# A decoder step on one core: twenty sample tokens taken out of the dense expert pass instead of sixteen, gate maps one to a chunk, and a shared projection for two query heads

## The chip, the cores and the metric

The kernel is one program on one core of one Trainium2 chip. The metric is the device time of one execution in microseconds (us); it is given as the median of the runs. The profile is one further execution, recorded by the hardware profiler. Its span runs from the first to the last instruction. All data are float32.

## What is computed

One layer of a decoder for two groups that share weights: 256 prompt tokens and 8 requests of 8 sample tokens, 320 tokens of width 2048 in all. Two attention mixers run side by side and share one output projection; cross-attention into 256 memory tokens follows; then the expert mixer, which takes more than half of the time. Cut to that mixer, for a block xb of tokens:

```python
q = (xb @ w_pq).reshape(TOKEN_BLOCK, PEER_HEADS, PEER_DKEY)        # 8 heads, 256 wide
s1 = jnp.einsum('thd,kd->thk', q[..., :half], sub_k1)              # 128 scores
s2 = jnp.einsum('thd,kd->thk', q[..., half:], sub_k2)
v1, i1 = lax.top_k(s1, PEER_TOPK); v2, i2 = lax.top_k(s2, PEER_TOPK)   # 16 and 16
cand = (v1[..., :, None] + v2[..., None, :]).reshape(..., PEER_TOPK * PEER_TOPK)
cidx = (i1[..., :, None] * PEER_NKEYS + i2[..., None, :]).reshape(...)
best, pos = lax.top_k(cand, PEER_TOPK)
eidx = jnp.take_along_axis(cidx, pos, axis=-1)                     # 16 of 16384 experts
gate = jax.nn.softmax(best.astype(jnp.float32), axis=-1)
act = jax.nn.gelu(jnp.einsum('td,thkd->thk', xb, expert_u[eidx]), approximate=False)
return jnp.einsum('thk,thkd->td', (gate * act).astype(xb.dtype), expert_v[eidx])
```

A token needs 8 x 16 = 128 experts, each a row of 2048 numbers (8 KB) in expert_u and one in expert_v. A residual add and a final RMSNorm close the layer. The outputs are both groups' results and the updated key and value buffers.

## The kernel before

It is written in raw blocks, one instruction list for each engine: SP issues the weight loads, POOL (GpSimd) the cache loads and the gathers, and PE, ACT and DVE compute. The order on each engine is the order of the code. Engines meet at counting semaphores: `x.wait_ge(s, n)` holds up that engine's whole list.

**Two token groups.** FIRST_TILE is the first 128 tokens; THE_REST is the other 192. **Weights** are streamed in pieces of 1 MB (128 x 2048 numbers) through `WR`, a ring of four slots. PE multiplies 16 stationary tiles of 128 x 128 out of each piece. A piece is loaded into its slot as soon as PE has used the piece that was there.

**Stages in order.** The memory projection and the input projection of all 320 tokens. Prompt attention in 16 steps, one pair of heads a step (`step_p` on DVE, `exp_p` and `turned_p` on ACT, `turn_p` on PE), over two probability buffers. Sample attention, one request after another (`softmax_s`, `turn_s`, `values_s`), with the output projection of FIRST_TILE, its cross-attention and its `co` tiles between the requests; at each request DVE adds the finished tiles to the stream (`add_to_stream`) after that request's softmax. Then the same stages for THE_REST (`out_tile`, `cq_tile`, its cross-attention over steps `it`, `co_tile`), with the query projection `pq_tile(0, f)` of FIRST_TILE between them. The order of tiles, and of the weight pieces with them, is the list `TILES`. A tile of `pq` for FIRST_TILE has 128 columns and one for THE_REST 192, and each `pq` piece is loaded twice. The memory keys and values of the requests are loaded by SP between weight pieces (`mem_keys`, `mem_values`): 2 MB of keys and 2 MB of values for requests 0 to 3, and as much again for 4 to 7.

**The expert mixer, by two methods.** For FIRST_TILE the chosen experts are gathered. One gather by POOL brings a "row": 128 expert rows, one to a partition, 1 MB. DVE takes its dot product with the tokens in `h_tok` (`u_dot`) or adds it, weighted, to the stream (`v_row`). There are 128 rows for these tokens (`SLOTS`) and, for the first `FEW` = 16 tokens of THE_REST, 16 more. So `ROWS` = 144 rows of expert_u and then 144 of expert_v go through rings of three buffers (`URING`) and four (`VRING`). For the other `DENSE` = 176 tokens every expert is computed: 128 chunks of 128 experts, with 16 matmuls each (`dense_u`, 176 columns wide) and a GELU by ACT, and then 128 chunks of expert_v (`dense_v`). Between the two, each token's gates are multiplied in. For four tokens at a time DVE writes one-hot matrices (`one_hots`), ACT weighs them, PE makes four gate maps (`gate_maps`), DVE applies the map to the chunks that are done (`apply_gates`), and ACT copies the rest (`s_gcp`).

**What stands where.** ACT's loop `dense_gelu` runs to chunk `EXPS` = 64 and takes the exponentials of the gates there; it runs on to `TAIL` = 80, where ACT waits for the gates and issues 8 small loads that spread the few tokens' choices over the partitions; then to `MAP_LO` = 100. PE has four output banks in turn, so that chunk c waits for the GELU of chunk c - 4. PE transposes the choices at chunk `TURN` = 92. DVE does 141 rows (`ROWS_BEFORE`) ahead of the gate maps, with a part of the choice of experts (`choose_part`, 18 parts for THE_REST) every third row from row 50 on. The 44 maps fall in chunks 100 to 123 (`chunk_of`). From chunk 100 on DVE does two rows at every third chunk and one at the others (`rows_with`).

The lines that open each half of the expert mixer for DVE:

```python
def u_dot(n):
    dve.wait_ge(s_ug[n % URING], 16 * (n // URING + 1))
def v_row(n):
    dve.wait_ge(s_vg[n % VRING], 16 * (n // VRING + 1))
```

## Time and profile before

| | us |
|---|---|
| median of 3 runs | 2312.56 (2309.89 to 2315.29) |
| the profiled execution | 2311.11 |
| its span | 2309.2 |
| PE busy, share of the span | 96% |
| DVE busy | 51% |
| bytes moved | 843.21 MB, mean 365 GB/s |

The profiled execution spends 1.9 us outside its span and lies 1.45 us below the median of the runs. A busy PE does not say that PE sets the pace: its matmuls overlap, and their ends are modelled. The number of instructions in a stretch says more. A float32 matmul stands as two instructions in the trace, so a piece of weights, or a chunk, is 32 of them. The stages in the trace: input projection until 397 us, prompt attention until 463, sample attention until about 660, THE_REST's projections and cross-attention until 905, its query projection until 997, chunks of expert_u until 1659 (the gate maps from 1485 to 1640), chunks of expert_v until 2293, and the final sums.

### The profile page before, as it was taken

The page shows a single profiled execution, that of the slowest core. Times are in us where ns is not written, and L with a number is a line of the kernel's source. Part 1 is how long each engine was busy: PE and PEld are TensorE (multiplying, and loading weights), DVE is VectorE, ACT ScalarE, POOL GpSimd, SP SyncE. Part 2 cuts the span into 40 slices and gives each one's busy share as a digit, 9 for nine tenths or more (in the row PEclk, how much of TensorE's full clock was granted, in tenths as well). Part 3 has the DMA queues.
Part 4 walks back from the last instruction along what each step waited for, and adds up shares of the span by engine and source line. Part 5 has one row for each costly group of instructions (what it writes and reads, how often), then busy time and mean ns, then how long its engine had stood idle before and what let it go on. Part 6 is the DMA issues. An engine that isn't in the chain of part 4 may idle for free.

```text
span 2309.2 us, 35404 instructions
## 1 busy us (share of the span) xinstructions
PE 2207.9 (96%) x14282; PEld 2015.7 (87%) x14282; DVE 1179.1 (51%) x2095; ACT 301.2 (13%) x926; POOL 386.3 (17%) x414
## 2 busy tenths in 40 slices
PE   7999998789889879999999999999999999999998
PEld 5677776577589868999999999899999999999998
DVE  3200003833566647767777544599744444444422
ACT  2000001722221012011111110144200000000000
POOL 0100000022302011232212221133311111111100
PEclk9999999999999989999999999999999999999999
DMA  7999982289959898999999999999999999999974
GB/s 280 405 413 381 385 316 81 80 333 357 398 201 396 345 383 315 407 398 422 422 421 420 420 420 420 372 372 376 402 422 421 422 422 421 422 422 422 421 315 155
DMA packets 117787, 843.21 MB, mean 365 GB/s; under 512 B 14432, under 2 KB 16608, under 8 KB 30656
## 3 DMA queue, kind: packets, MB, share of 16 engines
q1 hardware_dynamic: 62752, 485.30, 52.4%
q0 software_dynamic: 54128, 354.58, 37.7%
q10 hardware_dynamic: 816, 2.11, 0.2%
q8 instruction: 58, 0.95, 0.2%
q14 instruction: 33, 0.27, 0.0%
HBM read 834.25 MB, written 74.78 MB: 394 GB/s over the span
## 4 chain that ended last, share of the span: by engine, by line
PE 64%; DMA 23%; DVE 8%; issue 2%; ACT 1%; POOL 1%; SPq 0%; DVEq 0%; POOLq 0%; ACTq 0%
PE low L1414 39%; PE big L1414 24%; DMA BIG<-expert_u,VB 20%; DVE BIG L1240 4%; DMA WR<-wall 1%; DMA BIG<-kaT 1%; ACT BIG L630 1%; DMA BIG<-expert_v,VB 1%; DMA BIG<-memT 0%; DMA BIG<-va 0%; DVE CST L968 0%; POOL BIG L525 0%; DVE BIG L846 0%; PE low L1538 0%; DVE HT L883 0%
## 5 line engine op out<-in xcount | busy, mean ns | idle before, releaser
L1414 PE MATMUL low<-HT,WR 128*128 128x176 f32 (+3 forms) x6336 | 1081.9, 333 | 8.4 <-DMA WR<-wall 7.0
L1414 PEld LDWEIGHTS low<-HT,WR 128*128 128x128 f32 x6336 | 984.2, 191 | 98.2 <-issue 9.7
L1414 PE MATMUL big<-BIG,WR 128*128 (+3 forms) x2888 | 450.7, 312 | 11.3 <-DVE XT L891 7.1
L1253 DVE SCALAR_TENSOR_TENSOR XT<-BIG,VB,XT 128x2048 f32<-128x2048 f32 x128 | 300.9, 2351 | 302.7 <-DMA BIG<-expert_v,VB 302.4
L1414 PE MATMUL low<-BIG,WR 128*128 (+3 forms) x2616 | 434.8, 321 | 12.6 <-DMA WR<-wall 10.3
L1414 PEld LDWEIGHTS big<-BIG,WR 128*128 128x128 f32 x2888 | 419.3, 193 | 30.1 <-issue 18.5
L1240 DVE SCALAR_TENSOR_TENSOR BIG<-BIG 128x2048 f32<-128x2048 f32 x144 | 329.5, 2291 | 210.8 <-DMA BIG<-expert_u,VB 209.7
L1414 PEld LDWEIGHTS low<-BIG,WR 128*128 128x128 f32 x2616 | 411.0, 192 | 17.8 <-issue 10.5
L539 POOL DMA_INDIRECT BIG<-expert_u,VB x144 | 161.5, 1122 | 683.8 <-DVE BIG L1240 609.5
L545 POOL DMA_INDIRECT BIG<-expert_v,VB x144 | 161.5, 1122 | 558.2 <-DVE XT L1253 477.3
L914 DVE TENSOR_SCALAR BIG<-low 128x320 f32 x32 | 15.7, 492 | 264.0 <-PE low L1414 264.0
L1414 PE MATMUL big<-BIG 128*32 128x256 f32 (+4 forms) x868 | 80.5, 376 | 16.1 <-issue 8.9
L1414 PEld LDWEIGHTS big<-BIG 128*32 128x32 f32 (+2 forms) x868 | 52.7, 141 | 36.5 <-issue 14.6
L777 ACT ACTIVATE BIG<-low 128x176 f32 x100 | 31.8, 318 | 334.3 <-PE low L1414 324.2
L819 ACT ACTIVATE HT<-XT 128x2048 f32<-128x2048 f32 x1 | 1.9, 1910 | 557.1 <-DVE XT L1253 557.1
L793 ACT ACTIVATE HT<-HT,VB 128x128 f32<-128x128 f32 x176 | 56.2, 390 | 89.9 <-DVE HT L1354 89.9
L1354 DVE TENSOR_TENSOR HT<-CST,VB 128x512 f32<-128x512 f32 x88 | 56.6, 684 | 7.7 <-PE big L1414 7.7
L1414 PE MATMUL big<-HT 128*128 128x128 f32 x352 | 47.9, 280 | 5.0 <-ACT HT L793 5.0
L1414 PEld LDWEIGHTS big<-HT 128*128 128x128 f32 x352 | 45.5, 194 | 5.6 <-issue 5.5
L511 POOL DMA_DIRECT2D HT<-kbT x1 | 0.5, 536 | 266.8 <-PE low L1414 266.8
L525 POOL DMA_DIRECT2D BIG<-kaT x56 | 29.8, 539 | 81.2 <-PE low L1414 81.2
L622 ACT ACTIVATE BIG<-low 128x512 f32<-128x512 f32 (+3 forms) x5 | 2.3, 466 | 293.3 <-PE low L1500 293.3
(230 smaller groups left out, 1124.0 us busy)
## 6 DMA issues: line engine op xcount, KB each, us to landing
WR<-uT SPq DMA_DIRECT2D x128, 1024.0 KB
WR<-expert_v SPq DMA_DIRECT2D x128, 1024.0 KB
WR<-wall SPq DMA_DIRECT2D x122, 1024.0 KB
BIG<-va POOLq DMA_DIRECT2D x48, 512.0 KB, 11.0
BIG<-kaT POOLq DMA_DIRECT2D x64, 384.0 KB, 11.0
BIG<-kmT SPq DMA_DIRECT2D x2, 2048.0 KB, 12.9
BIG<-vm SPq DMA_DIRECT2D x8, 512.0 KB, 13.4
XT<-xT SPq DMA_DIRECT2D x1, 2560.0 KB, 21.9
```

The source lines that it names most:

```text
L525: pool.dma_start(kr[j][:, NEWK:SW], d["kaT"][n, j, :, FIRST:PAST]).then_inc(s_kr[j], 16)
L539: nc.gpsimd.indirect_dma_start(u_ring[n % URING], None, d["expert_u"], bass.IndirectOffsetOnAxis(eidx[:, n:n + 1], 0)).then_inc(s_ug[n % U ...
L545: nc.gpsimd.indirect_dma_start(v_ring[n % VRING], None, d["expert_v"], bass.IndirectOffsetOnAxis(eidx[:, v_slot(n):v_slot(n) + 1], 0)).the ...
L622: nc.scalar.activation(VT[0:m, t, q * 512:q * 512 + w], bank[3 + n % 2][0:m, 0:w], ACT.Copy).then_inc(s_vtev, 1)
L630: ins = nc.scalar.activation(pb[:, s, lo:hi], pb[:, s, lo:hi], ACT.Exp, bias=stat[:, c:c + 1], scale=1.0, accum_out=stat[:, c + 4:c + 5])
L777: nc.scalar.activation(C[:, bass.ds(i * (UB * DENSE) + r * DENSE, DENSE)], u_out[r], ACT.Gelu).then_inc(s_dev, 1)
L793: nc.scalar.activation(x, x, ACT.Copy, scale=turned[2][:, 4 * g + j:4 * g + j + 1]).then_inc(s_weighed, 1)
L914: nc.vector.tensor_scalar(QK[:, bass.ds(i * (4 * NT) + r * NT, NT)], bank[r % 2][:, 0:NT], 1.0, None, ALU.mult).then_inc(s_ev, 1)
L1240: nc.vector.scalar_tensor_tensor(out=u, in0=u, scalar=1.0, in1=h_tok if n < SLOTS else h_few, op0=ALU.mult, op1=ALU.mult, accum_out=dots[: ...
L1253: nc.vector.scalar_tensor_tensor(out=x_tok, in0=rows_of(row), scalar=weight, in1=x_tok, op0=ALU.mult, op1=ALU.add).then_inc(s_vsum, 1)
L1354: ins = nc.vector.tensor_tensor(hot[z][g % 2], iota.unsqueeze(1).broadcast_to([P, 4, NKEY]), turned[z][:, 4 * g:4 * g + 4].unsqueeze(2).br ...
L1414: return nc.tensor.matmul(out, lhsT, rhs, start=start, stop=stop, skip_group_check=True)
```

## The change

**More tokens gathered.** `FEWER` = 4 more tokens leave the dense pass: `DENSE` is 172 (`ALONE` = 20 tokens are gathered), and `ROWS` is 148. The 128 experts of each of the four tokens are laid out as four rows, with (quarter of the 16 choices, head, token) on the partitions. ACT issues four small loads for each head beside the one that was there: 40 in place of 8. Before row 144 PE transposes 16 blocks of the four tokens into `h_tok`, four blocks at each of chunks 92 to 95. The sums of the four go through `h_few` once more, after PE has added the first sixteen; that addition stands at V chunk 32 instead of 96, and the second one at 96. In the V half the four rows are rows 56 to 59.

**Gate maps.** They fall in chunks 80 to 122, one for each chunk after its last matmul, over three banks instead of four. `EXPS`, `TAIL` and `TURN` are 56, 64 and 72. DVE does 118 rows ahead of the maps, with two of the 18 parts in every five rows, and weighs the gates at row 98 instead of 106.

**Heads 6 and 7.** The four `pq` tiles 12 to 15 are computed for all 320 tokens at once, ahead of THE_REST's other twelve. Of the tiles 10 to 15 that stood in and behind the cross-attention of THE_REST, only 10 stands in it and 11 behind `co`.

**Memory loads.** The first keys and values are issued three weight pieces later; half of the second values get room of their own and go out with them.

**Prompt and sample attention.** DVE negates the row maxima (which lets ACT start its exponentials) ahead of the multiplications that normalize the pair before, and there is a third probability buffer from the sixth pair on. In the sample attention DVE adds the tiles that PE finished beside the scores ahead of the next softmax, and FIRST_TILE's `co` tiles from the seventh on rotate over three banks.

```diff
-EXPS, TAIL = 64, 80
-TURN = 92
-MAP_LO, MAP_HI = 100, 124
+EXPS, TAIL = 56, 64
+TURN = 72
+MAP_LO = 80
+E2_AT = 92
 MAPS = DENSE // 4
+MAP_HI = MAP_LO + MAPS
-ROWS_BEFORE = 141
+ROWS_WEIGH = 98
+ROWS_BEFORE = 118
...
-         + tiles_of("cq", 1, 0, 4) + tiles_of("pq", 0, 10, 14) + tiles_of("co", 1, 0, 16) + tiles_of("pq", 0, 14, 16)
-         + tiles_of("pq", 1, 0, 16))
+         + tiles_of("cq", 1, 0, 4) + tiles_of("pq", 0, 10, 11) + tiles_of("co", 1, 0, 16) + tiles_of("pq", 0, 11, 12)
+         + tiles_of("pq", 1, 12, 16) + tiles_of("pq", 1, 0, 12))
...
-                if before == POS["out", 1, 15]:
+                if before == POS["cq", 1, 0]:
                     sp.wait_ge(s_used, FREED["out", 1, 15])
                     mem_keys(0)
-                    mem_values(0)
+                    mem_values(0, 0, 4)
+                    sp.wait_ge(s_sc, 3)
+                    sp.wait_ge(s_idx, 3)
+                    mem_values(1, 0, 2)
...
             for h in range(PH):
-                act.dma_start(chosen[FEW * h:FEW * (h + 1), :, SLOTS:ROWS], few_src[:, :, h * PK:(h + 1) * PK]).then_inc(s_few, 16)
+                act.dma_start(chosen[FEW * h:FEW * (h + 1), :, SLOTS:SLOTS + FEW], few_src[:, :, h * PK:(h + 1) * PK]).then_inc(s_few, 16)
+                for part in range(PARTS):
+                    to, k = (part * PH + h) * FEWER, h * PK + part * FEWER
+                    act.dma_start(chosen[to:to + FEWER, :, SLOTS + FEW:ROWS], fewer_src[:, :, k:k + FEWER]).then_inc(s_few, 16)
...
-                if n + 1 < REQ:
-                    softmax_s(n + 1)
-                for f in (*with_scores, *with_turn):
+                for f in with_scores:
                     add_to_stream(FIRST_TILE, CROSS, f)
...
+                if n + 1 < REQ:
+                    softmax_s(n + 1)
+                for f in with_turn:
+                    add_to_stream(FIRST_TILE, CROSS, f)
...
-                if last:
-                    dve.wait_ge(s_dv, mr)
-                    nc.vector.tensor_scalar(pl[:, 0, 0:256], pl[:, 0, 0:256], rd[:, 0:1], None, ALU.mult)
-                    nc.vector.tensor_scalar(pl[:, 0, 256:384], pl[:, 0, 256:384], rd[:, 1:2], None, ALU.mult).then_inc(s_nrm, 1)
...
-                if n % 3 == 0 and later:
+                if (n - ROWS_AHEAD) % 5 in (0, 2) and later:
                     choose_part(*later.pop(0))
...
+            v_chunks(MAP_LO, FEWER_OUT)
+            pe.wait_ge(s_vsum, FEWER_AT + FEWER)
+            for k in range(KT):
+                mm(v_all[k][:, FEW:ALONE], h_few[:, k * P:(k + 1) * P], pick_fewer, start=False, stop=True)
+            v_chunks(FEWER_OUT, NCH - WR_N)
```

The small loads on ACT, in the row of the list at `TAIL`. Before:

```order
L777 ACTIVATE BIG<-low 128x176
L774 REGISTER_ALU
L774 COMPARE_AND_BRANCH
L786 DMA VB<-HT 16x2x16 x8
L774 UNCONDITIONAL_BRANCH
```

After:

```order
L813 ACTIVATE BIG<-low 128x172
L810 REGISTER_ALU
L810 COMPARE_AND_BRANCH
L822 DMA VB<-HT 16x2x16
L825 DMA VB<-HT 4x2x4 x4
```

The last two rows stand eight times in a row before the next loop of GELUs, where one row of eight loads stood.

SP's loads from the output projection to the first chunk of expert_u: weight pieces (`WR<-wall`), memory keys (`kmT`) and values (`vm`). Before:

```order
L484 DMA WR<-wall 128x2048 x51
L460 DMA BIG<-kmT 128x4x1024
L464 DMA BIG<-vm 128x1024 x4
L484 DMA WR<-wall 128x2048 x7
L460 DMA BIG<-kmT 128x4x1024
L484 DMA WR<-wall 128x2048 x2
L464 DMA BIG<-vm 128x1024 x4
L484 DMA WR<-wall 128x2048 x20
```

After:

```order
L517 DMA WR<-wall 128x2048 x54
L490 DMA BIG<-kmT 128x4x1024
L494 DMA BIG<-vm 128x1024 x6
L517 DMA WR<-wall 128x2048 x4
L490 DMA BIG<-kmT 128x4x1024
L517 DMA WR<-wall 128x2048
L494 DMA BIG<-vm 128x1024 x2
L517 DMA WR<-wall 128x2048 x17
```

Weight pieces come to 76 instead of 80, the first memory loads stand three pieces later, and two of the second four values stand ahead of the second keys.

PE from the last `co` tile of THE_REST to the first chunks of expert_u (`low<-HT,WR` are `pq` tiles, 16 matmuls to a tile). Before:

```order
L1414 MATMUL low<-HT,WR 128x128 x16
L1414 MATMUL big<-BIG,CST 128x192
L1414 MATMUL low<-HT,WR 128x128 x16
L1414 MATMUL big<-CST,BIG 128x128 x4
L1414 MATMUL low<-HT,WR 128x192 x32
L1766 MATMUL big<-CST,BIG 128x128 x16
L1414 MATMUL low<-HT,WR 128x192 x224
L1414 MATMUL low<-CST,BIG 128x128 x8
L1414 MATMUL big<-CST,BIG 128x128 x16
L1414 MATMUL low<-HT,WR 128x176 x64
```

After:

```order
L1472 MATMUL big<-BIG,CST 128x192
L1472 MATMUL low<-HT,WR 128x128 x16
L1472 MATMUL big<-CST,BIG 128x128 x4
L1472 MATMUL low<-HT,WR 128x320 x32
L1829 MATMUL big<-CST,BIG 128x128 x16
L1472 MATMUL low<-HT,WR 128x320 x32
L1472 MATMUL low<-HT,WR 128x192 x32
L1472 MATMUL big<-CST,BIG 128x128 x4
L1472 MATMUL low<-HT,WR 128x192 x160
L1472 MATMUL low<-CST,BIG 128x128 x8
L1472 MATMUL big<-CST,BIG 128x128 x16
L1472 MATMUL low<-HT,WR 128x172 x64
```

One tile of 128 columns is gone from here, and four of the sixteen tiles of 192 columns have become tiles of 320. Three more tiles of 128 columns are gone from the cross-attention ahead of it.

## Rows read from the trace of the kernel before

**Rows 1.** The page's 40 slices: granted clock, and busy share of the DMA engines.

```profile
PEclk9999999999999989999999999999999999999999
DMA  7999982289959898999999999999999999999974
```

**Rows 2.** Stretches of the expert mixer: busy times with instruction counts, clock, DMA share, GB/s.

```profile
core 0: us, PE busy (x) PEld busy (x) DVE busy (x) ACT busy (x) POOL busy (x), PEclk, DMA share, GB/s
997.00:1302.00 305.00, 305.00 (x2047) 305.00 (x2047) 222.14 (x486) 41.16 (x80) 71.88 (x59) 1.00 1.01 417
...
1490.00:1640.00 150.00, 149.92 (x1089) 149.63 (x1089) 140.47 (x180) 63.91 (x255) 49.51 (x30) 1.00 0.92 360
1659.00:2219.00 560.00, 559.73 (x3631) 541.78 (x3630) 263.85 (x114) 1.80 (x3) 102.38 (x109) 1.00 1.01 422
2222.00:2292.00 70.00, 70.00 (x472) 70.00 (x471) 2.80 (x10) 4.56 (x12) 0.00 (x0) 1.00 0.50 182
```

**Rows 3.** Groups by line, 997 to 1302 and 1659 to 2219 us: busy us, mean ns, idle before.

```profile
L1240 DVE SCALAR_TENSOR_TENSOR BIG<-BIG 128x2048 f32<-128x2048 f32 x59 | 135.3, 2294 | 76.7 <-DMA BIG<-expert_u,VB 75.8
...
L1253 DVE SCALAR_TENSOR_TENSOR XT<-BIG,VB,XT 128x2048 f32<-128x2048 f32 x112 | 263.3, 2351 | 295.4 <-DMA BIG<-expert_v,VB 295.4
```

**Rows 4.** The chain that ended last, whole tiles of it: start us, us, what.

```profile
75.96 292.87 PE low L1414 x1088
...
693.97 5.20 PE low L1414 x32
...
834.56 3.57 PE low L1414 x32
```

**Rows 5.** Timeline of DVE in one prompt step: start us, us, what.

```profile
432.47 0.34 DVE L978 TENSOR_SCALAR BIG<-BIG,CST 128x256 f32<-128x256 f32 x1
...
432.93 0.15 DVE L985 SCALAR_TENSOR_TENSOR CST<-CST 128x4 f32<-128x4 f32 x1
...
436.90 0.15 DVE L985 SCALAR_TENSOR_TENSOR CST<-CST 128x4 f32<-128x4 f32 x1
```

**Rows 6.** Waits of PE, 510 to 560 and 560 to 610 us: total us, times, longest.

```profile
PE big L1414 <- DVE XT L891: 7.1, 2, 3.5
...
PE big L1414 <- DVE HT L1073: 3.5, 1, 3.5
```

**Rows 7.** Stretches of 20 us, columns as in rows 2.

```profile
520.00:540.00 20.00, 19.31 (x189) 15.61 (x189) 6.21 (x26) 2.73 (x9) 4.17 (x8) 0.91 0.90 341
540.00:560.00 20.00, 16.47 (x124) 16.19 (x121) 3.90 (x12) 2.06 (x8) 3.23 (x7) 0.83 0.89 359
...
800.00:820.00 20.00, 13.01 (x64) 12.74 (x63) 5.25 (x7) 0.00 (x0) 0.94 (x1) 0.74 0.95 379
860.00:880.00 20.00, 12.32 (x63) 9.01 (x64) 7.60 (x14) 2.19 (x5) 5.15 (x4) 0.70 0.88 348
1480.00:1500.00 20.00, 15.05 (x95) 14.81 (x94) 15.87 (x30) 7.39 (x27) 0.94 (x1) 0.83 0.72 279
```

**Rows 8.** Timeline of PE, three waits: start us, us, what, [idle before <-releaser].

```profile
808.65 9.61 PE L1414 MATMUL low<-HT,WR 128*128 128x192 f32 x41 [6.99 <-DMA WR<-wall]
...
865.12 3.64 PE L1414 MATMUL big<-BIG 128*32 128x512 f32 x16 [8.89 <-issue]
...
1485.50 2.05 PE L1414 MATMUL big<-HT 128*128 128x128 f32 x8 [4.95 <-ACT HT L793]
```

**Rows 9.** Timeline of ACT at its DMA issues, columns as in rows 8.

```profile
77.29 0.39 ACTq L613 DMA_DIRECT2D mk_out<-BIG  x1
77.72 0.67 ACTq L614 DMA_DIRECT2D mv_out<-BIG  x1
...
1379.26 5.26 ACTq L786 DMA_DIRECT2D VB<-HT  x8
1384.82 0.32 ACT L777 ACTIVATE BIG<-low 128x176 f32 x1 [5.39 <-issue]
```

**Rows 10.** Groups by line, 1490 to 1640 us, columns as in rows 3.

```profile
L1354 DVE TENSOR_TENSOR HT<-CST,VB 128x512 f32<-128x512 f32 x82 | 52.8, 684 | 6.2 <-PE big L1414 6.2
...
L1364 DVE TENSOR_TENSOR BIG<-BIG,big 128x404 f32<-128x404 f32 (+22 forms) x43 | 26.4, 613 | 0.9 <-PE big L1414 0.9
```

More of the change, by code:

```diff
@@ L223, in build @@
         VTF = QK[:, T_VA * NT:T_IN * NT]
-        probs_p = VTF[:, 0:1536].rearrange("p (b s c) -> p b s c", b=2, s=2)
+        probs_two = VTF[:, 0:1536].rearrange("p (b s c) -> p b s c", b=2, s=2)
+        q_pairs = [QK[:, (T_QA + 2 * i) * NT:(T_QA + 2 * i + 2) * NT].rearrange("p (s t) -> p s t", s=2) for i in range(2)]
         probsT_p = VTF[:, 1536:2304].rearrange("p (s c) -> p s c", s=2)
@@ L293, in build, with probs_p @@
         x_tok = XT_by[:, :, 0:P]
+        def probs_p(p):
+            buffer = p % 2 if p < OF_THREE else (2, 1, 0)[(p - OF_THREE) % 3]
+            if buffer == 2:
+                return q_pairs[0][:, :, 0:256], q_pairs[1][:, :, 0:P]
+            return probs_two[:, buffer, :, 0:256], probs_two[:, buffer, :, 256:384]
         def rows_of(x):
@@ L1148, in _ @@
                 if n == 4:
[L1149 to L1150 removed]
+                    keep_cross_query(FIRST_TILE, 1)
+                    keep_cross_query(FIRST_TILE, 2)
+                if n + 1 < REQ:
+                    softmax_s(n + 1)
+                for f in with_turn:
+                    add_to_stream(FIRST_TILE, CROSS, f)
+                if n < 3:
+                    for f in range(max(5 * n - 1, 0), 5 * n + 4):
+                        group_square(FIRST_TILE, CROSS, f)
+                if n == 4:
+                    keep_cross_query(FIRST_TILE, 3)
                 if n in (5, 6):
@@ L1906, in dense_v @@
                         pe.wait_ge(s_dev, NCH - UB + k // 2 + 1)
-                    ins = mm(v_all[k][:, FEW:REST], WR[:, slot_of(r) * D + k * P:slot_of(r) * D + (k + 1) * P], coefs, start=(first and k % 2 == 0), stop=last)
+                    ins = mm(v_all[k][:, ALONE:REST], WR[:, slot_of(r) * D + k * P:slot_of(r) * D + (k + 1) * P], coefs, start=(first and k % 2 == 0), stop=last)
                     if last:
```

201 lines of the change are left out of this document (124 added, 77 removed).

## The prediction

> **What bounds the kernel now.** I read the 40 slices first, then the expert mixer stretch by stretch, then the waits inside the stretches. The slices show the clock at its full level nearly everywhere and the DMA engines full in most of the second half [rows 1]. Two resources are at their limit at once, and the question for each stretch is which of them gives way.
>
> A chunk is 32 matmul instructions. In the U half (997 to 1302 us) 2047 of them take 305 us, so a chunk takes 4.77 us. At the very end, when the gathers are over, 472 take 70 us [rows 2]: 4.75 us. There DMA is half idle, so this is PE's own pace; 176 columns in two passes at 2.4 GHz make 146.7 ns an instruction and 4.69 us a chunk, and I use 4.70 with about 0.07 for the loop in U. In the V half 3631 instructions take 560 us, 4.93 us a chunk, beside 112 rows at 560 / 112 = 5.0 us [rows 2, 3]. DMA is full there at 422 GB/s, and DVE waits for gathers for 295 us. Chunk and row bring 1.0486 MB each, and 2 x 1.0486 MB / 422 GB/s = 4.97 us: the two streams share evenly, one piece each every 4.97 us, while both ask. In the U half a row comes every 305 / 59 = 5.17 us, because DVE also chooses experts, and PE gets what it asks for.
>
> So a narrower chunk pays where PE sets the pace, and pays nothing in V while rows flow. The rows end at about 2220 us and PE at 2293: the rows have 70 us to spare.
>
> **Chunk width.** Four columns fewer are 16 x 2 x 4 x 2 / 2.4 = 107 ns less a chunk. Tiles of 128, 192 and 320 columns take 3.57, 5.20 and 292.87 / 34 = 8.61 us [rows 4]: 25.5 ns a column between the first two and 26.6 between the last two, so 102 to 107 ns for four. I take 107.
>
> The Trainium skill, "TensorE: Matmul & The Clock Gate", section "Back-to-back issue gap", says that the spacing of matmuls is set by the weight load and the matmul together, so that narrow ones gain less than their columns. In its extreme, the four columns would gain nothing here; the slope between 128 and 192 columns speaks against it. It is rival (d).
>
> **Prompt attention.** A step's cycle (negated maxima, exponentials, DVE again) takes 436.90 - 432.93 = 3.97 us [rows 5]. The two multiplications that start 432.93 - 432.47 = 0.46 us ahead of the negation leave the cycle, and then DVE's own list is nearly full. I take 0.4 us for 13 of 16 steps, -5; bounds 0 (DVE's list is the cycle) and 16 x 0.46 = -7. The third buffer only keeps a wait from coming in.
>
> **Sample attention.** PE waits 7.1 us in two places for additions, and 3.5 us in one for query copies, that DVE does behind a softmax [rows 6]; after two of them the clock is 0.91 and 0.83 [rows 7], at half speed for 9% and 17% of 40 us of windows' time, which costs 2 x 20 x 0.13 = 5 us at most. Moved ahead, that is up to -15. But DMA is busy 0.90 and 0.89 in the same stretches, so only some 4 us of transfers can move up before the cache loads are late; beyond that the wait changes its name. I take -6, bounds -3 and -15. The `co` tiles over three banks: -1.
>
> **Cross-attention of THE_REST.** PE stands 6.99 us for a weight piece queued behind 4 MB of memory loads, and 8.89 us for the second values [rows 8]; the clock is 0.74 and 0.70 there [rows 7], some 5 us more. The loads now stand three pieces later, so the first wait goes. But three tiles (3 x 3.57 = 11 us) that filled waits are taken out of the steps, and what is late next is known: one `pq` piece now stands behind 5 MB of memory loads, the second values come behind nearly the same bytes as before, and DVE does a row in each of nine steps, at about 5 us each. I take half of the 21 us: -11, bounds 0 and -21.
>
> **Query projection.** Four tiles of 320 and twelve of 192 columns (34.4 + 62.4 = 96.8 us) for sixteen of 192 (83.2): +13.6. One tile of 128 less behind `co`, whose place is partly a wait for the square sum: -2. Net +12. The four pieces that are no longer loaded twice give DMA time to rows, not to PE.
>
> The U half starts at 997 - 5 - 6 - 1 - 11 + 12 = 986.
>
> **U chunks 0 to 79.** Width: 80 x 0.107 = -8.6. Rows and chunks at the new pace ask for a little more than 421 GB/s: +2. Then the small loads. ACT's eight took 5.26 us, 0.66 each, in which it did no GELU [rows 9]. Forty take 26.3. PE may run four chunks ahead, 4 x 4.66 = 18.7 us, so with 0.9 us for two GELUs it stops for 8.5 us at chunk 68; the eight of before were covered by the same four chunks. The stop of 4.95 us at the first map [rows 8] lowered the clock to 0.83 of 20 us [rows 7], 2 us of PE's work; so +10.5. Bounds: 40 x 0.39 = 15.6 us, by ACT's cheapest issue [rows 9], would be covered and cost 0; 40 x 0.67 is what I took. Two issues of 512 KB, the second 0.67, and eight of 2 KB at 0.66 agree, so size doesn't set it, and I take the dear end. Sum +4: chunk 80 is reached 11 - 4 = 7 us earlier than before.
>
> The Trainium skill, "DMA: Bandwidth & Descriptors", section "Issuing engines are not separate DMA queues", calls the sequencer's time to issue a DMA usually small beside the DMA itself. By that this term would be nothing; the rows of ACT show it as large as a fifth of the four chunks that cover it. It is rival (a).
>
> **Chunks 80 to 127.** Chunk 80's GELU stands at 1384.8 [rows 9] and V starts at 1659, so these 48 took 278 us with chunk 80 itself. The stop of 4.95 us goes: DVE has its 118 rows ahead of chunk 80 (row 98 waits for the exponentials at chunk 56, and twenty rows at 4.97 us end near chunk 76), and the first map stands at a chunk's end. The maps' stretch ran 150 us with 1089 instructions [rows 2], of which a map has eight: about 23.4 chunks of 32 and 43 maps, so a map costs (150 - 23.4 x 4.70) / 43 = 0.93 us. PE alone needs 43 x (4.60 + 0.93) + 5 x 4.6 = 261 us. DVE needs 2 x 0.6 for one-hots, 0.6 for a map [rows 10], 0.2 for the late gates and 1.33 x 2.35 for rows, 5.1 us a chunk. DMA is the tightest: one chunk and 1.33 rows are 2.33 pieces at 2.49 us, 5.8 us. The 30 rows of expert_u, with a ring of three, come a little slower; 6.0. So 22 x 6.0 + 21 x 5.8 + 5 x 4.8 = 278, as before: 0. Bounds: 261, and 318 if rows come every 4.97 us.
>
> **V half.** Before, 634 us: 128 x 4.70 = 602 by PE and 32 by sharing with about 113 rows. After: 128 x 4.60 = 589, and 112 rows at 4.97 - 4.60 = 0.37, 41; 630 in all, -4. Row 56 waits for the first addition at V chunk 32, which the 33 rows done before V put nine chunks later than its turn. The chunks run at 4.60 meanwhile, and the rows' spare time shrinks from 70 to about 30 us. That cover makes it free; it would cost up to 42 us without it.
>
> Sum: -11 + 4 + 0 - 4 = -11. The profiled execution, 2311.1, becomes 2300, and the median lies 1.45 us above it, 2301.6. Since I took the dear end for the small loads and the ring, I lean 2.6 us lower: **2299 us** as median.
>
> **The rivals.**
> (a) The small loads cost ACT less, as each carries less. No stop at chunk 68: -10.5, **2288.5**. For it the lone issue at 0.39, against it the two sizes that agree [rows 9].
> (b) The rows set the pace of the maps, in place of the stop. If one keeps coming every 4.97 us, a chunk takes 6.6 us and chunks 80 to 127 318 us: +40, **2339**, slower. It decides from about 4.6 us a row on, where 13 us are lost in 48 chunks. For it: three buffers turned in 3 x 5.17 us in the U half [rows 2, 3]. Against: PE takes less than its half there and leaves more.
> (c) The memory loads are late in another place and the cross-attention gives nothing: +11, **2310**.
> (d) PE's pace does not follow the columns: U and V give nothing, +8.6 + 4, **2312**.
>
> **How the numbers follow.** Forecast 0.45, (a) 0.22, (b) 0.12, (c) 0.13, (d) 0.03, and 0.05 for several terms at their better bounds, about 2278. The range is to hold 8 in 10: from 2284, below (a), to 2314, above (c) and (d); (b) and the last case stay out. A measurement can tell about 0.2% here, 4.6 us, so faster means below 2308. Nearly all of the forecast (0.42), (a), the last case and a third of (c) make 0.73; the same gets 0.14; slower 0.13, nearly all of it (b).
>
> **What the profile would show.** Instructions of 172 columns 143 ns apart; forty issues of ACT in one piece near 26 us, and PE idle for about 8 us soon after; the first map without a wait; chunks 80 to 122 at 5.8 to 6.0 us with DVE waiting for gathers; U starting near 986; rows ending some 30 us before PE. The forecast is wrong if rows in the maps come slower than 4.6 us each, if PE waits in the cross-attention as long as before, or if rows end last.

## The result, and the profile after

Before 2309.82 us, after 2316.55 us (medians of 20 runs each): ratio 1.003, 95% interval 1.0022 to 1.0038. The change makes the kernel slower by 0.3%, where I had forecast 2299 us and a gain. The profiled execution of after has a span of 2315.3 us (2317.55 us as time), that of before 2309.2.

The first view is stretch by stretch, with the columns of [rows 2]: U before the stop of PE, that stop, the maps, V while the rows wait, V while they flow, the tail.

```profile
987.00:1287.00 300.00, 299.67 (x2045) 297.67 (x2044) 214.33 (x473) 43.24 (x85) 68.34 (x55) 1.00 0.99 409
1287.00:1320.00 33.00, 20.89 (x142) 20.63 (x142) 15.62 (x14) 1.16 (x5) 6.45 (x6) 0.84 1.01 413
1500.00:1640.00 140.00, 136.39 (x970) 135.46 (x970) 111.05 (x125) 36.03 (x153) 34.28 (x31) 1.00 1.00 408
...
1800.00:1830.00 30.00, 30.00 (x204) 30.00 (x203) 5.16 (x3) 0.00 (x0) 3.50 (x2) 0.94 0.65 242
1855.00:2135.00 280.00, 276.63 (x1819) 265.27 (x1818) 133.15 (x57) 0.00 (x0) 52.45 (x56) 1.00 1.01 422
2262.00:2292.00 30.00, 30.00 (x207) 30.00 (x207) 3.40 (x2) 2.30 (x3) 0.00 (x0) 1.00 0.62 233
```

Against [rows 2]: 32 instructions in U take 4.69 us by the first row, 4.77 before; 4.64 by the last, 4.75 before. From 1855 to 2135 us they take 280 / 1819 x 32 = 4.93 us, exactly as before, beside 57 rows at 4.91. So the narrower chunk pays where PE sets the pace, and it pays nothing where PE shares DMA with the rows.

The boundaries, in the timeline of PE after: the first head projection, behind the sample attention (658.00; before 670.27), the one behind THE_REST's `co` tiles (876.78; 896.83), U (987.54; 997), the first map (1383.33, no wait; before 1485.50 with 4.95 us), V (1652.53; 1658.79).

```profile
658.00 4.17 PE L1472 MATMUL low<-HT,WR 128*128 128x128 f32 x35 [0.67 <-ACT BIG L630]
...
876.78 3.73 PE L1472 MATMUL low<-HT,WR 128*128 128x128 f32 x32
...
987.54 12.71 PE L1472 MATMUL low<-HT,WR 128*128 128x172 f32 x86
...
1383.33 1.05 PE L1472 MATMUL big<-HT 128*128 128x128 f32 x8
...
1652.53 2.50 PE L1472 MATMUL big<-BIG,WR 128*128 128x172 f32 x16
```

Counted in chunks (32 instructions each; us at the start of the first one, counted in the two traces):

| reached | before | after | after - before |
|---|---|---|---|
| U chunk 0 | 996.9 | 987.5 | -9.4 |
| U chunk 64 | 1302.4 | 1288.6 | -13.8 |
| U chunk 80 | 1378.8 | 1378.7 | -0.1 |
| V chunk 0 | 1658.8 | 1652.5 | -6.3 |
| V chunk 8 | 1697.8 | 1705.2 | +7.4 |
| end of span | 2309.2 | 2315.3 | +6.1 |

So the kernel is ahead by 14 us, loses it between chunks 64 and 80, gains 6 in the maps and loses 14 in the first eight chunks of V. Behind each loss stands a stop of PE: one wait behind the first, three close together behind the second. The first, in the timelines of ACT and of PE: forty issues in one piece from 1289.03 to 1318.5, and PE idle for 12.11 us.

```profile
1289.03 0.77 ACTq L822 DMA_DIRECT2D VB<-HT  x1
1289.83 3.23 ACTq L825 DMA_DIRECT2D VB<-HT  x4
...
1314.11 4.43 ACTq L825 DMA_DIRECT2D VB<-HT  x4
1319.15 0.93 ACT L813 ACTIVATE BIG<-low 128x172 f32 x4 [29.97 <-issue]
...
1319.52 10.73 PE L1472 MATMUL low<-HT,WR 128*128 128x172 f32 x59 [12.11 <-ACT BIG L813]
```

The second stands at the start of V. A chunk that is computed after some of the maps gets its GELU for the mapped tokens into a buffer of its own (the late GELU, L849), and DVE multiplies it onto the gates (L1428, the late gates); there is one such buffer, so that the next late GELU waits for DVE. PE's first matmuls of V write into the banks that held the last four chunks of U, so they need the late GELUs of all four. In the timelines of PE, ACT and DVE: PE waits for the late GELUs, these for the late gates, and these stand behind a row (L1307) whose gather arrives every 5 us. The first line here is from the waits of 1640 to 1680 us and gives PE's three waits together; before, the only one there is 0.2 us.

```profile
PE low L1472 <- ACT CST L849: 11.0, 3, 5.6
```

```profile
1661.84 1.52 PE L1472 MATMUL low<-BIG,WR 128*128 128x172 f32 x4 [4.11 <-ACT CST L849]
1668.98 1.51 PE L1472 MATMUL low<-BIG,WR 128*128 128x172 f32 x4 [5.63 <-ACT CST L849]
...
1661.47 0.32 ACT L849 ACTIVATE CST<-low 128x172 f32<-128x172 f32 x1 [4.65 <-DVE BIG L1428]
1668.62 0.32 ACT L849 ACTIVATE CST<-low 128x172 f32<-128x172 f32 x1 [6.83 <-DVE BIG L1428]
...
1658.77 2.35 DVE L1307 SCALAR_TENSOR_TENSOR XT<-BIG,VB,XT 128x2048 f32<-128x2048 f32 x1 [2.37 <-DMA BIG<-expert_v,VB]
1661.04 0.33 DVE L1428 TENSOR_TENSOR BIG<-BIG,CST 128x172 f32<-128x172 f32 x1
1663.42 4.85 DVE L1307 SCALAR_TENSOR_TENSOR XT<-BIG,VB,XT 128x2048 f32<-128x2048 f32 x2 [2.05 <-DMA BIG<-expert_v,VB]
1668.19 0.33 DVE L1428 TENSOR_TENSOR BIG<-BIG,CST 128x172 f32<-128x172 f32 x1
```

At 1652.5 PE has done chunk 127 of U; DVE multiplies chunk 125's gates at 1661.04, on which chunk 126's GELU waits, and chunk 126's at 1668.19. V's first chunk takes 17.8 us and its second 6.9, at a clock of 0.66 (below), instead of 4.7 each.

How far behind this work is can be read from the trace: from the start of a chunk's last matmul to its late GELU it is 4.0 us at chunk 99, 7.8 at 104, 13.0 at 106, between 7.9 and 14.3 from there to chunk 126, and 16.2 at 127. In the kernel before it is never over 4.7. DVE has done 28 rows of `expert_v` when V starts, where its list has 33 ahead of the last late gates; it does the other five first, from 1653.8 to 1670.8 us.

### The profile page after: what moved, and what is told of

Read it like the earlier page. It is cut to its first block, busy times and chain, and to the rows that moved or that the text cites. A ratio compares the mean times of both kernels' runs of the same rounds, so it can differ in the third digit from the quotient of the medians.

```text
span 2315.3 us, 35254 instructions
## 1 busy us (share of the span) xinstructions
PE 2193.3 (95%) x14194; PEld 1985.5 (86%) x14194; DVE 1199.2 (52%) x2126; ACT 294.9 (13%) x940; POOL 394.1 (17%) x422
## 4 chain that ended last, share of the span: by engine, by line
PE 71%; DMA 17%; DVE 6%; issue 3%; ACT 2%; ACTq 1%; POOL 1%; SPq 0%; DVEq 0%; POOLq 0%
PE low L1472 51%; PE big L1472 19%; DMA BIG<-expert_v,VB 5%; DMA BIG<-expert_u,VB 5%; DMA BIG<-kaT 4%; DMA WR<-expert_v 1%; DVE BIG L1291 1%; DMA WR<-wall 1%; ACTq L825 1%; ACT BIG L663 1%; POOL BIG L558 1%; DMA BIG<-va 0%; DMA BIG<-memT 0%; DVE CST L1014 0%; DVE BIG L1305 0%
## 5 line engine op out<-in xcount | busy, mean ns | idle before, releaser
L1472 PE MATMUL low<-HT,WR 128*128 128x172 f32 (+3 forms) x6232 | 1071.8, 334 | 22.4 <-ACT BIG L813 12.1
L1472 PEld LDWEIGHTS low<-HT,WR 128*128 128x128 f32 x6232 | 964.4, 191 | 122.1 <-ACT BIG L813 12.4
L1307 DVE SCALAR_TENSOR_TENSOR XT<-BIG,VB,XT 128x2048 f32<-128x2048 f32 x128 | 301.0, 2352 | 307.1 <-DMA BIG<-expert_v,VB 306.9
L1472 PE MATMUL low<-BIG,WR 128*128 (+3 forms) x2616 | 429.6, 319 | 22.0 <-ACT CST L849 11.0
L1472 PE MATMUL big<-BIG,WR 128*128 (+3 forms) x2888 | 441.2, 308 | 5.0 <-DMA WR<-expert_v 1.6
L1472 PEld LDWEIGHTS big<-BIG,WR 128*128 128x128 f32 x2888 | 413.3, 192 | 22.2 <-issue 22.1
L1291 DVE SCALAR_TENSOR_TENSOR BIG<-BIG 128x2048 f32<-128x2048 f32 x148 | 338.1, 2290 | 151.7 <-DMA BIG<-expert_u,VB 150.4
L572 POOL DMA_INDIRECT BIG<-expert_u,VB x148 | 176.6, 1193 | 704.4 <-DVE BIG L1291 612.4
L578 POOL DMA_INDIRECT BIG<-expert_v,VB x148 | 154.4, 1044 | 586.7 <-DVE XT L1307 471.3
L1472 PE MATMUL big<-BIG 128*32 128x256 f32 (+4 forms) x868 | 82.7, 380 | 14.2 <-issue 3.6
L813 ACT ACTIVATE BIG<-low 128x172 f32 x80 | 24.7, 314 | 276.1 <-PE low L1472 245.9
L1305 DVE SCALAR_TENSOR_TENSOR BIG<-BIG,VB 128x2048 f32<-128x2048 f32 x18 | 42.3, 2351 | 13.0 <-DMA BIG<-expert_v,VB 12.5
```

Of the source, the lines that this page charges most:

```text
L572: nc.gpsimd.indirect_dma_start(u_ring[n % URING], None, d["expert_u"], bass.IndirectOffsetOnAxis(eidx[:, n:n + 1], 0)).then_inc(s_ug[n % U ...
L578: nc.gpsimd.indirect_dma_start(v_ring[n % VRING], None, d["expert_v"], bass.IndirectOffsetOnAxis(eidx[:, v_slot(n):v_slot(n) + 1], 0)).the ...
L813: nc.scalar.activation(C[:, bass.ds(i * (UB * DENSE) + r * DENSE, DENSE)], u_out[r], ACT.Gelu).then_inc(s_dev, 1)
L1291: nc.vector.scalar_tensor_tensor(out=u, in0=u, scalar=1.0, in1=h_few if SLOTS <= n < SLOTS + FEW else h_tok, op0=ALU.mult, op1=ALU.mult, a ...
L1305: nc.vector.scalar_tensor_tensor(out=h_few, in0=row, scalar=weight, in1=h_few, op0=ALU.mult, op1=ALU.add).then_inc(s_vsum, 1)
L1307: nc.vector.scalar_tensor_tensor(out=x_tok, in0=rows_of(row), scalar=weight, in1=x_tok, op0=ALU.mult, op1=ALU.add).then_inc(s_vsum, 1)
```

## The experiments

Ratios are to the kernel before, run beside each on the same chip (its medians there: 2308.5 to 2311.3 us). Differences from the changed kernel's 2316.55 us are between medians taken beside 2309.82 and beside these, and carry that 1 or 2 us with them. Every kernel but the first and one other, which says so, starts from the changed one.

**The attention part alone.** The kernel before with all edits up to U: `probs_p` and `step_p`, the order in the sample steps, the memory loads, `co` over three banks, and this order of tiles; `FEW = 16`, `DENSE` and the maps stay.

```
+         + tiles_of("cq", 1, 0, 4) + tiles_of("pq", 0, 10, 11) + tiles_of("co", 1, 0, 16) + tiles_of("pq", 0, 11, 12)
+         + tiles_of("pq", 1, 12, 16) + tiles_of("pq", 1, 0, 12))
```

> The kernel before with only the attention changes (third softmax buffer and earlier normalization, sample additions ahead of the softmax, memory loads moved, heads 6 and 7 projected for both groups); still 16 gathered tokens, 176 columns, the maps from chunk 100. Theory: the early gain is real and reaches the end of the kernel, because nothing behind it changed: U starts near 987 us instead of 997, and the time is 9 us shorter, 2301 us. Rival: the early gain is given back later in any case (the gathers or the choice of experts start no earlier and the first map waits for them), the time is 2308 us or more, and the loss of the changed kernel does not come from its expert mixer alone.

Measured 2292.78 us, ratio 0.992 (0.9902 to 0.9939): twice the expected gain. PE in its trace:

```profile
985.36 4.94 PE L1445 MATMUL low<-HT,WR 128*128 128x176 f32 x32
...
1468.27 1.27 PE L1445 MATMUL big<-HT 128*128 128x128 f32 x8 [0.61 <-ACT HT L818]
...
1639.51 2.55 PE L1445 MATMUL big<-BIG,WR 128*128 128x176 f32 x16
```

U starts 11.5 us earlier, and PE waits 0.61 us at the first map where it waited 4.95 [rows 8]; with the clock that fell after it, chunk 100 takes 6.8 us instead of 13.1. V starts 19.3 us earlier. The rows of `expert_u` had got ahead by more than U: DVE starts row 104 at 1271 us, 1296 before. So the early part is worth 18 us in this kernel, and the rest of the change (the four gathered tokens with the new place of the maps) costs 2316.55 - 2292.78 = 24 us.

**One row a chunk at the end.** From chunk 112 on, DVE does one row a chunk instead of four rows in three chunks.

```
 def rows_with(c):
-    return 2 if c % 3 == 0 else 1
+    return 2 if c % 3 == 0 and c < 112 else 1
```

> The changed kernel, but from chunk 112 on DVE takes one gathered row a chunk instead of four rows in three chunks. Theory: PE stands 11 us at the start of V because the last late gates queue in DVE behind rows whose gathers come every 4.97 us; with five rows fewer DVE is not behind, the waits at 1657 to 1669 us and the half clock after them go, V chunk 1 takes 5 us instead of 17.8; about 4 of the 15 us come back later because chunks loaded ahead during the stop are no longer there. Time 2316.5 - 11 = 2305 us. Rival: DMA is nearly full during the stop (share 0.92), so what PE loses there the streams gain, and removing it gives at most 2 us: 2315 us.

Measured 2305.80 us, ratio 0.9972 (0.9959 to 0.9986), 10.8 below the changed kernel. V starts without a wait:

```profile
1653.87 2.50 PE L1472 MATMUL big<-BIG,WR 128*128 128x172 f32 x16
1656.20 2.50 PE L1472 MATMUL low<-BIG,WR 128*128 128x172 f32 x16
```

The late GELU comes 4.4 us behind at chunk 118 and 0.3 from chunk 123 on, where the changed kernel has 12.3 and up to 16.2. So the stop's mechanism is shown, and also that a part of it comes back: with the stop, V's chunks 2 to 14 take 4.7 us out of the filled ring of `WR`; without it they take 5.0 to 5.1 from chunk 3 on.

**The small loads spread.** 

```
             act.wait_ge(s_gates, 3)
-            for h in range(PH):
-                ... (five issues)
-            dense_gelu(TAIL, MAP_LO)
+            for c, heads in (((64, 68), (0, 1)), ((68, 72), (2, 3)), ((72, 76), (4, 5)), ((76, 80), (6, 7))):
+                for h in heads:
+                    ... (five issues)
+                dense_gelu(*c)
```

> The changed kernel, but the forty small loads that ACT issues in one piece before chunk 64's GELU are issued ten at a time before chunks 64, 68, 72 and 76. Theory: PE's stop of 12.1 us at chunk 68 is the length of the forty issues (30 us) less the four chunks PE may run ahead; ten issues take 7 us and are covered; the stop and the half clock behind it go, chunk 80 is reached 14 us earlier, and the time is 2316.5 - 14 = 2302 us. Rival: the stop only gave DVE the time to have its 118 rows done, so it comes back as a wait at the first map: 2312 us or more.

Measured 2301.83 us, ratio 0.9967 (0.9954 to 0.998), 14.7 below the changed kernel. Ten issues take 7.3 us, and PE works through (ACT's issues, then PE):

```profile
1285.13 0.75 ACTq L823 DMA_DIRECT2D VB<-HT  x1
1285.91 3.22 ACTq L826 DMA_DIRECT2D VB<-HT  x4
...
1292.62 0.31 ACT L813 ACTIVATE BIG<-low 128x172 f32<-128x172 f32 x1 [7.34 <-issue]
...
1269.81 52.37 PE L1473 MATMUL low<-HT,WR 128*128 128x172 f32 x358
```

**Both.** The last two edits together.

> Both of the last two edits at once. Theory: the two stops are separate and their gains add: 2316.5 - 11 - 14 = 2291 us, faster than both kernels. Rival: rows come earlier behind one another, the gathers bound the last chunks anyway, and only the larger gain stays: 2302 us.

Measured 2288.27 us, ratio 0.99 (0.9881 to 0.9919), 28.3 below the changed kernel; 10.8 + 14.7 = 25.5 were to be had by the two alone. Within the intervals they add, and together they are no less than the 24 us that separate the changed kernel from its attention part. Between this kernel and that with the attention part alone the intervals overlap, so it stays open whether four more gathered tokens are worth anything once both stops are mended; by the medians, about 4 us.

Six or so executions leave a median uncertain by some 4 us, and part of this comes in ahead of the expert mixer: in the profiled executions of the changed kernel and of those made from it U starts anywhere from 985.0 to 992.9 us, though their lists are the same up to there. Counted from the start of U, one execution each:

| us | start of U to chunk 80 | chunk 80 to V | V to the end | in all |
|---|---|---|---|---|
| before | 381.9 | 280.0 | 650.4 | 1312.3 |
| changed | 391.1 | 273.9 | 662.7 | 1327.7 |
| attention part alone | 381.9 | 272.3 | 650.3 | 1304.5 |
| one row a chunk | 391.6 | 271.7 | 654.6 | 1318.0 |
| loads spread | 375.5 | 276.4 | 660.0 | 1311.9 |
| both | 376.5 | 274.3 | 653.9 | 1304.7 |

Each edit works where it is meant to: the loads between U and chunk 80, the rows in V. By this count both together give 23.0 us.

**How much of the issues is covered.** The changed kernel with 25 loads in one piece before chunk 64 and 15 before chunk 72 (the same loop, with heads 0 to 4 before `dense_gelu(64, 72)` and 5 to 7 before `dense_gelu(72, 80)`).

> The changed kernel (nothing else mended), with 25 small loads in one piece before chunk 64's GELU and 15 before chunk 72's. Theory: the stop is the length of the issues less the four chunks of lead; 25 x 0.67 = 16.8 us is under 18.7 - 0.9 = 17.8 us, so PE does not stop behind chunk 67, or by less than 1 us, and the one execution is near 2302 us. Rival: PE has less lead than four chunks at that point (ACT stands behind DVE or behind loads), and it stops for 3 us or more.

One execution: 2304.29 us, so that only its trace is read here. PE runs through the place where it stood 12.11 us; the 25 issues begin at 1291.57 and end with the last line here.

```profile
1291.57 0.75 ACTq L823 DMA_DIRECT2D VB<-HT  x1
...
1306.38 2.69 ACTq L826 DMA_DIRECT2D VB<-HT  x4
...
1287.76 40.90 PE L1473 MATMUL low<-HT,WR 128*128 128x172 f32 x279
```

17.5 us of issues are covered by four chunks of 4.67, 18.7. The stop is the length of the issues less the lead of PE: 29.5 - 18.7 = 10.8 us for the changed kernel, and 1.0 us more from the last issue to the first matmul behind the GELU (1318.54 to 1319.52); measured 12.1.

**The wait of the rows.** On both mends, `FEW_OUT` at 16 instead of 32. In the changed kernel POOL has no gather to issue for 40 us, because row 56 waits for the first addition:

```profile
1826.19 3.00 POOL L578 DMA_INDIRECT BIG<-expert_v,VB  x1 [39.99 <-DVE BIG L1303]
```

> The kernel of the last run (one row late, loads spread), but the sixteen tokens' sums are added at V chunk 16 instead of 32, so that row 56 does not wait for it. Theory (as the prediction had it): the wait of the rows, 17 us there, is covered; while it lasts the chunks run at 4.7 instead of 5.0 us, and without it the rows end some 17 us earlier and that much more of the tail runs at 4.7; the time is the same, 2288 us, within 2. Rival: the rows' wait leaves DMA half idle, and that capacity is missing later: 2280 us or less.

Measured 2286.53 us, ratio 0.9903 (0.9886 to 0.992), the lowest median here, and within the interval of the kernel with the two mends. POOL's wait for that row, in the waits of 1700 to 1900 us, first of the kernel with both mends, then of this one:

```profile
POOL BIG L578 <- DVE BIG L1304: 21.0, 1, 21.0
```

```profile
POOL BIG L578 <- DVE BIG L1304: 3.0, 1, 3.0
```

18 us of waiting removed move the median by 1.7 us, and V to the end from 653.9 to 651.9 us in the two traces: the rows' spare time covers the wait, as the prediction had said.

**The additions between wide matmuls.** Each addition of gathered sums is 32 narrow matmul instructions in one piece; in the changed kernel there are two of them. The timeline of PE at both, with the wide matmuls behind them:

```profile
1820.85 1.85 PE L1472 MATMUL low<-VB,BIG 128*128 128x16 f32 x16
1822.56 1.94 PE L1472 MATMUL big<-VB,BIG 128*128 128x16 f32 x16
1824.34 4.22 PE L1472 MATMUL big<-BIG,WR 128*128 x16
1828.36 2.57 PE L1472 MATMUL low<-BIG,WR 128*128 x16
1830.77 2.50 PE L1472 MATMUL big<-BIG,WR 128*128 x16
1833.10 2.50 PE L1472 MATMUL low<-BIG,WR 128*128 x16
...
2140.04 1.84 PE L1472 MATMUL low<-VB,BIG 128*128 128x4 f32 x16
2141.74 2.84 PE L1472 MATMUL big<-VB,BIG 128*128 128x4 f32 x16
2144.44 4.93 PE L1472 MATMUL big<-BIG,WR 128*128 x16
2149.17 2.60 PE L1472 MATMUL low<-BIG,WR 128*128 x16
```

Sixteen wide ones take 1833.10 - 1830.77 = 2.33 us at the full clock; the sixteen after the first addition take 4.02 and those after the second 4.73. So the first costs 3.5 + 1.7 = 5.2 us on PE and the second 4.4 + 2.4 = 6.8. The edit, on both mends:

```
+                    for i, k in enumerate(LAST_ORDER):
+                        ... (one wide matmul of the chunk)
+                        if i % 4 == 1:
+                            f = 4 * (c - c0) + i // 4
+                            ins = mm(v_all[f][:, cols], h_few[:, f * P:(f + 1) * P], picked, start=False, stop=True)
```

> One row late, loads spread, and the two additions of gathered sums no longer stand as sixteen narrow matmuls in one piece: one of them stands behind every fourth wide one, over four chunks (32 to 35, 96 to 99). Theory: each addition costs 6.4 us, of which 3.5 is its 32 instructions and 2.9 the clock that falls to half during or after them; between wide matmuls the clock does not fall, and the time is 2288 - 6 = 2282 us. Rival: the cost is only that of the instructions (and of switching to other weights), which stay the same in number: 2288 us.

Measured 2290.49 us, ratio 0.9914 (0.9897 to 0.993): the 6 us expected did not come; a gain of 2 or 3 could not be told. The clock did stay full at both additions, at the first as the first of these rows shows (1790 to 1820 us of this kernel, with the columns of [rows 2]; the second row is the changed kernel at its first addition):

```profile
1790.00:1820.00 30.00, 29.96 (x214) 29.70 (x213) 1.11 (x1) 0.00 (x0) 0.00 (x0) 1.00 0.70 271
```

```profile
1820.00:1830.00 10.00, 10.00 (x66) 10.00 (x66) 5.16 (x3) 0.00 (x0) 3.50 (x2) 0.83 0.40 138
```

The four chunks that hold an addition take 5.6 us, 0.93 more each, 3.7 in all. That the 1.5 and 3.1 us saved do not reach the end in full would fit the sharing, but no run separates it: DMA goes on while PE is held up by the addition, the next chunks take 4.7 us out of what it has brought, and behind the second addition there are 13 of these in a row with the hold-up and 8 without, before they take 5.0. Also the first addition now ends four chunks later, and row 56 with it (1819 against 1806 us). The same edit on the attention part alone, with its one addition:

> The kernel with only the attention changes (sixteen gathered tokens), and its one addition put between the wide matmuls of chunks 96 to 99. Theory: the addition cost 5.3 us and costs 3.6: 2292.8 - 1.7 = 2291 us; so with everything mended four more gathered tokens are worth about 9 us, not the 26 us that their columns take from PE in 256 chunks. Rival: where rows have ended nothing hides the narrow matmuls and the time stays 2293 us or more.

Measured 2293.41 us, ratio 0.993 (0.9912 to 0.9947), against 2292.78: the 1.7 us expected are less than these medians can tell. Of the expectation's 9 us for the four tokens nothing is confirmed.

**The transposes apart.** On both mends, `E2_AT = (90, 92, 94, 96)`. In the changed kernel the second group waits for ACT's copy of the first:

```profile
1459.81 1.04 PE L1960 MATMUL big<-CST,BIG 128*128 128x128 f32 x4 [2.70 <-ACT BIG L853]
1460.64 6.13 PE L1472 MATMUL low<-HT,WR 128*128 128x172 f32 x32
```

> One row late, loads spread, and the four groups of transposes of the four tokens stand behind chunks 90, 92, 94 and 96 instead of 92 to 95. Theory: PE waits at the second group for ACT's copy of the first, which stands behind ACT's gate work of its chunk, and the clock falls after it; chunks 92 to 95 take 28.8 us instead of 22.4; two chunks apart the copy is done in time, 1.8 us of transposes stay and 4.6 us go: 2284 us. Rival: the copies are late behind DVE's rows whatever the distance, and the wait only moves: 2288 us.

Measured 2290.00 us, ratio 0.9913 (0.9897 to 0.9929): no gain, as the rival said. The wait is gone from the list of PE's waits, and the transposes cost their chunks 1.8 us instead of 6.5. But chunks 106 to 109, where DVE turns from rows of `expert_u` to rows of `expert_v`, now take 28.4 us instead of 22.7. Other small stops are gone, and from chunk 80 to V it is 271.6 us against 274.3, so in the traces most of the gain is taken back and not all of it.

**All mends, and the next wait.** The five edits together.

> The changed kernel with all mends: loads spread, one row a chunk from 112 on, first addition at V chunk 16, additions between wide matmuls, transposes two chunks apart. Theory: from the run with the first three (2286.5 us) the spread additions take what the trace of V showed, 4 us, and the transposes 1 us (the stop at chunk 108, where ACT waits for the last dot, gave the rest back): 2281.5 us. Rival: each gain found so far ends in the next wait on the gathered rows, and the time stays at 2286 us or more.

Measured 2287.53 us, ratio 0.9899 (0.9882 to 0.9916): the rival. The stop at chunk 108, where that of the changed kernel is 6.6 us instead of 5.6, has grown to 10.2: PE waits 3.52 us for weighed one-hots; DVE stood 6.28 us at the first row of `expert_v` while the one-hots of the next maps were due (PE, then DVE).

```profile
1532.12 2.05 PE L1473 MATMUL big<-HT 128*128 128x128 f32 x8 [3.52 <-ACT HT L833]
...
1513.95 1.29 DVE L1304 TENSOR_SCALAR BIG<-BIG,VB 128x2048 f32<-128x2048 f32 x1 [6.28 <-DMA BIG<-expert_v,VB]
1515.15 1.29 DVE L1413 TENSOR_TENSOR HT<-CST,VB 128x512 f32<-128x512 f32 x2
```

With `ROWS_BEFORE = 120`:

> All mends, and 120 instead of 118 rows of expert_u ahead of chunk 80, since DVE stands idle before the first map. Theory: the last dot comes 1.5 chunks earlier, the stop at chunk 108 (about 4 us) shrinks, time 2 us below the run without it: 2279.5 us. Rival: DVE is not ready for the first map, PE stops there for 3 us or more, and the time is 2283 us or more.

Measured 2295.97 us, ratio 0.9938 (0.9922 to 0.9954): slower by 8.4 us than without it, well over the 2283 from which on the rival holds. But its stop does not stand mainly at the first map, as the rival has it: the longest wait, 4.12 us, is at chunk 105, and ahead of it DVE stands 4.63 us at its first row of `expert_v`. The profiled execution was the fastest of the six (2288.1 us; the others 2294.8 to 2296.8), and PE waits 7.1 us for one-hots in its maps where the kernel above waits 3.5. So the trace shows a direction, and the loss of the other five stays open in size and in cause.

With `elif c > DOTS_DONE + 1:` in place of `elif c > DOTS_DONE:`, so that the first row of `expert_v` is taken a chunk later:

> All mends, and DVE takes the first row of expert_v one chunk later, so that it does not stand 6.3 us at its gather with the one-hots of the next maps behind it. Theory: this is the same mechanism as the stop at the start of V (gate work queued in DVE behind a row that has not arrived); the stop at chunk 108 (10.2 and 7.5 us instead of 5.6 twice, 6.5 us) goes, and with it the gain of the transposes and of the additions comes through: 2287.5 - 6 = 2281.5 us. Rival: the rows are the bound of the last 48 chunks, one row fewer there is one row more in V, and the time stays at 2286 us or more.

Measured 2287.15 us, ratio 0.99 (0.9881 to 0.9919), the rival's range. That one wait shrinks from 3.52 to 1.92 us:

```profile
1529.74 1.27 PE L1473 MATMUL big<-HT 128*128 128x128 f32 x8 [1.92 <-ACT HT L833]
```

But PE's waits for one-hots in the maps come to 3.5 us as before, in four places instead of one. A gain of the 6 us expected would have shown. From the two mends on, five further edits were tried, alone or together; four left the median within 3 us of 2288.27, the fifth (120 rows) made it worse, and in the maps what one of them took from PE's waits mostly came up in another.

## Why the prediction was wrong

Against the profiled execution: 2300 said, 2317.6 measured. The step that failed is the V half, of which the prediction had the pace and not the wait at its start. By its own steps:

- **Up to U: right in sum, in part by luck.** Prompt attention -5 said, -3.1 measured (the negations of two steps, 428.12 and 431.77 us in DVE's timeline, stand 3.65 us apart, 3.97 before [rows 5]: 0.32 us a step and not 0.4, in half of the steps). Sample attention -7 with the banks: -9.2; the 3.5 us waits of [rows 6] are gone. Cross-attention -11: -7.8, but not by its mechanism. PE still stands 7.14 us for a weight piece and 3.67 + 3.55 us near the second values, against 6.99 and 8.89 [rows 8], and all its waits there come to 24 us, 23 before. That is the prediction's own sign of being wrong, "if PE waits in the cross-attention as long as before". What was gained is the work of the three tiles taken out (11 us), less a longer time at the lower clock. Query projection +12: +10.6. U starts at 987.5, said 986: errors of 2 to 3 us each way that cancel, in a place where executions differ by up to 8.
- **Chunk width: right.** 4.77 to 4.69 us a chunk in U and 4.75 to 4.64 in the tail, where -0.107 was said; nothing while rows flow. Rival (d) is out.
- **U chunks 0 to 79: right in mechanism, too small.** +4 said, +9.3 measured. The term that was mis-sized is the stop: 10.5 said. The forty issues took 29.5 us instead of 26.3 (their last piece of four 4.43), PE stood 12.1 instead of 8.5, and with the clock behind it the two chunks lost 16.9 + 6.6 - 2 x 4.67 = 14.2 us. The run with the loads spread gives 14.7. Rival (a) is out: the small loads are as dear as the second of the two large ones (0.67). The Trainium skill, "DMA: Bandwidth & Descriptors", section "Issuing engines are not separate DMA queues", calls that time usually small beside the DMA itself; here it is 0.74 us a load (29.5 / 40), and forty of them made the longest single wait of PE in the expert mixer.
- **Chunks 80 to 127: better than said.** 0 said, -6.1 measured (273.9 us against 280.0). A chunk with its map takes 5.6 us, PE's own pace (40 instructions; 970 take 140 us in the stretch from 1500 us, 5.77 each forty with the stops in it), not the 5.8 to 6.0 that I gave to DMA. The step left something out as well: it priced the four groups of transposes at nothing, and they cost 6.3 us with their wait. Rows came every 4.59 us here (58 from 1386.2 to 1652.5), right at the 4.6 that the prediction names as its limit, and this did not show in PE's pace but behind it, in V.
- **V: the step that failed.** -4 said; from the start of V to the end of the span it is 662.7 us against 650.4, +12.3, of which the first eight chunks have 13.7. I took the V half as paces and shares and looked at its row wait, but not at what its first matmuls wait for. I had worked out that DVE has 5.1 us of work a chunk and that rows come every 4.97 us, 1.33 of them a chunk, 6.6 us; I used that as a rival for the pace of all maps (b) and priced it at 40 us or nothing. It was neither. PE's pace held to the last chunk but for waits of 3.5 us in all, since it may run four chunks ahead of the late GELUs, and the lag came due in one piece where V needs them all. The prediction let the rows cost PE time only through the pace of the chunks, and took the overlap of the late gates with PE for free. In the kernel before, 44 maps in 24 chunks made most of these chunks 6.6 us long (1510.4 to 1612.9 us for sixteen), which is what 1.33 rows take; DVE kept up. Spread over 43 chunks the maps leave PE 5.6 us a chunk, and in the last four, without a map, 4.67. The lag did not grow evenly: its largest step, from 7.8 to 13.0 us, is at chunks 104 to 106, behind the 4.0 and 2.7 us that DVE stands at its first two rows of `expert_v`; after that DVE does not catch up, and from chunk 123 to 127 the lag goes from 7.9 to 16.2. The run with one row a chunk at the end shows 10.8 us for it.
- **The second addition** was not in the sum at all. It costs 6.8 us on PE. How much of that reaches the end is not shown: spreading both saved nothing that the medians can tell.
- **The rows' wait at V chunk 32: right.** Free, or nearly so: 18 us of it removed give about 2. The rows ended some 31 us before PE, said 30.
- **Slips in the working** that leave the sum as it is: a clock of 0.91 and 0.83 over 20 us means half speed for 17% and 34% of it and not for 9% and 17%; the 5 us follow from the right figures. The eight issues before were 5.26 of 19 us, more than a quarter of the four chunks that cover them and not a fifth.

U start +1.5, U chunks +5.3, maps -6.1, V +16.3 more than said make 17.0 of the 17.6 us. Without V the sum would have come out, and that by luck: the stop behind the small loads and the maps were off by 5 and 6 us in opposite directions.

One thing the sum could not have shown from its terms: the early part was worth 18 us to the kernel before, since its first map waited for rows, and rows gained more time than U. I had said that the four pieces no longer loaded twice give time to rows and not to PE; for the kernel before, giving time to rows was giving it to PE. Whether it is those pieces or the earlier start of the gathers is not told apart here.

## What to carry to other kernels

When an engine that may run ahead by a few buffers is made faster than the one that feeds it, the lag of the slow one does not show in the pace; look where the next stage needs all of it at once, and price the lag there. In an in-order engine, work that others wait for must not stand behind an operand that arrives by DMA at its own rate: three stops here (the start of V and chunk 108 of the changed kernel, the first map of the kernel before) were gate work of at most 0.7 us an instruction behind a row that had not come. And count issues of small DMAs on a computing engine as that engine's busy time, in pieces shorter than the lead of whoever waits for it.
